# Input of the first expert tile summed in PSUM instead of gathered, and tile tables by matmuls, in a one-core attention and mixture-of-experts block

## The reference

```
h = x + concat([conv, attn]) @ W_o            # gated short convolution, latent attention
n = RMSNorm(h)
top 4 of 32 experts by n @ w_router + b_router; gates = softmax of the four
y[token] = sum over its experts: gate * expert(n[token])
expert(r) = act(r @ w_gate_up + b) @ w_down + b_down ;  out = h + y
```

## Time and profile before

| what | value |
|---|---|
| three runs | 2205.37, 2206.23, 2207.76 us (median 2206.23) |
| profiled execution | 2206.78 us; its span 2205.0 us |
| PE busy | 2078.0 us, 94% of the span |
| granted PE clock, mean | 0.976 of full speed |

### The profile page before, as it was taken

One profiled execution on the slowest core, in us unless ns is written; L12 is line 12 of the kernel. 1 busy time (PEld: TensorE's weight loads), 2 busy tenths in 40 slices (PEclk: granted clock), 3 DMA queues, 4 the chain that ended last, 5 costly groups with the idle time before them and its releaser, 6 DMA issues.

```text
span 2205.0 us, 41908 instructions
## 1 busy us (share of the span) xinstructions
PE 2078.0 (94%) x15574; PEld 1883.0 (85%) x15575; DVE 738.2 (33%) x1949; ACT 443.7 (20%) x1078; POOL 563.1 (26%) x645
## 2 busy tenths in 40 slices
PE   7999999999968899999999999999999999999991
PEld 6777777745538899999999999999999999999991
DVE  1322333233443334234333333333233332343331
ACT  1333323232311111111111111111111111111110
POOL 2211111100233223322222322323223233232321
PEclk9999999999978999999999999999999999999996
DMA  7100000242517889999899999999999999999987
GB/s 251 40 10 11 10 11 1 80 131 47 145 39 228 268 281 310 313 297 304 270 305 277 310 289 298 310 284 289 301 312 318 308 272 283 321 315 319 306 284 88
DMA packets 305892, 486.97 MB, mean 221 GB/s; under 512 B 105920, under 2 KB 127200, under 8 KB 305792
## 3 DMA queue, kind: packets, MB, share of 16 engines
q1 hardware_dynamic: 247184, 437.28, 60.6%
q0 software_dynamic: 33376, 45.11, 9.9%
q10 hardware_dynamic: 25280, 3.85, 1.1%
HBM read 454.83 MB, written 35.84 MB: 223 GB/s over the span
## 4 chain that ended last, share of the span: by engine, by line
PE 91%; issue 2%; DVE 2%; ACT 1%; DMA 1%; POOL 1%; ACTq 0%; DVEq 0%; SPq 0%; POOLq 0%
PE psum L1003 43%; PE psum L1019 22%; PE psum L803 8%; PE psum L952 5%; PE psum L842 3%; PE psum L911 2%; PE psum L820 2%; PE psum L910 1%; PE psum L884 1%; PE psum L932 1%; PE psum L895 1%; DMA area<-in_w_in 1%; PE psum L982 1%; DVE area L1302 0%; DVE area L1297 0%
## 5 line engine op out<-in xcount | busy, mean ns | idle before, releaser
L1003 PE MATMUL psum<-area 128*128 128x128 f32 (+3 forms) x8192 | 980.2, 282 | 37.0 <-issue 18.9
L1003 PEld LDWEIGHTS psum<-area 128*128 128x128 f32 x8192 | 971.6, 192 | 42.4 <-issue 42.4
L1019 PE MATMUL psum<-area 128*128 128x128 f32 (+3 forms) x4096 | 496.4, 282 | 0.9
L1019 PEld LDWEIGHTS psum<-area 128*128 128x128 f32 x4096 | 484.5, 191 | 10.0 <-DVE area L1302 8.7
L1283 DVE TENSOR_SCALAR area<-psum,area 128x160 f32<-128x160 f32 x256 | 86.4, 380 | 615.6 <-PE psum L1003 615.6
L600 POOL DMA_INDIRECT sum_rows<-area x165 | 264.0, 1600 | 67.4 <-issue 40.2
L762 ACT ACTIVATE area<-area 128x320 f32<-128x320 f32 x128 | 60.4, 472 | 735.8 <-DVE area L1283 735.6
L803 PE MATMUL psum<-area 128*128 128x128 f32 x1536 | 176.8, 276 | 10.5 <-ACT area L681 4.0
L803 PEld LDWEIGHTS psum<-area 128*128 128x128 f32 x1536 | 173.3, 192 | 15.3 <-ACT area L677 5.8
L590 POOL DMA_INDIRECT area<-normed_rows,area x165 | 161.3, 977 | 61.5 <-issue 61.5
L585 POOL TENSOR_TENSOR area<-area 128x5 uint32<-128x5 uint32 x33 | 6.3, 190 | 617.4 <-DVE area L1268 590.4
(11 more groups left out here) (184 smaller groups left out, 1250.6 us busy)
## 6 DMA issues: line engine op xcount, KB each, us to landing
area<-in_w_gate_up SPq DMA_DIRECT2D x256, 1024.0 KB, 6.4
area<-in_w_down SPq DMA_DIRECT2D x128, 1024.0 KB
area<-in_w_in SPq DMA_DIRECT2D x3, 2048.0 KB, 21.5
area<-in_x SPq DMA_DIRECT2D x9, 512.0 KB, 4.0
area<-in_w_o SPq DMA_DIRECT2D x1, 4096.0 KB, 13.0
sum_rows<-area SPq DMA_DIRECT2D x32, 128.0 KB
normed_rows<-area SPq DMA_DIRECT2D x8, 512.0 KB, 3.1
out<-sum_rows SPq DMA_DIRECT2D x4, 1024.0 KB, 14.0
```

Of the source, the lines that this page charges most:

```text
L1003: ins = mm(dst, w_gu[piece][:, k, c * P:(c + 1) * P], xT[:, PART * s + k, 0:width], start=(s == 0 and k == 0 and c % 2 == 0), stop=(s == 1 ...
L1019: ins = mm(bank[4 + d // 3][:, (d % 3) * SLOTS:(d % 3) * SLOTS + width], w_dn[q][:, kk, d * P:(d + 1) * P], actT[:, 2 * q + kk, 0:width], ...
```

## The change

Tile 0 is now always expert 0's first tile (`levels` and `floor` see to that when it is empty), and its input is no longer gathered from DRAM after the tables. Three parts are summed in PSUM banks 4 to 6, already transposed: rows of blocks 0 to 5, read from DRAM early by two indirect gathers with list entries read while block 7 is in work, and multiplied by the identity (`GTa`, `GTb`); and rows of blocks 6 and 7, straight from SBUF, multiplied by a 0/1 matrix that says which token takes which slot (`XTa`, `XTb`, `XT`). ACT and DVE copy the sum into `xT`. The last block's rows get a buffer of their own, `hf_last`, made after the `HB` copy. The last block's `places`, and with it POOL's list writes, come after the tables. The number of tiles an expert needs comes from a comparison with a row of levels, and the sums over experts from one matmul with a triangular 0/1 table, `upto`. The semaphore `gathered` becomes one for each of the five gathers. SP's branch on the first expert goes, and the early weights signal PE's semaphores themselves.

```diff
-                    ("HA", e), ("HB", e), ("RT", e), ("RK", e)]
+                    ("HA", e), ("XTa", e - 1), ("HB", e), ("XTb", e - 1), ("RT", e), ("GTa", e), ("RK", e), ("GTb", e), ("XT", e)]
...
                 b = i % H_ROWS
+                if i == NT - 1:
+                    sp.wait_ge(listed, 16 * (NT - DIRECT) * TOPK)
+                    for c, (a, m) in enumerate(FIRST):
+                        sp.dma_start(early_list[0:m, c, :], lists[a:a + m, :]).then_inc(early_in, 16)
...
+            wait(pv_done, NT * HEADS)
+            for c, (a, m) in enumerate(FIRST):
+                g.memset(early_rows[c][0:m, :], 0.0).then_inc(early_picked, 1)
             for n in range(NT):
+                if n == NT - DIRECT:
+                    wait(early_in, 16 * 2)
+                    for c, (a, m) in enumerate(FIRST):
+                        g.tensor_scalar(early_pick[0:m, c:c + 1], early_list[0:m, c, 0:1], 1.0 / Q, None, ALU.mult).then_inc(early_picked, 1)
+                    wait(early_picked, 2 + len(FIRST))
+                    wait(hf_out, 16 * (NT - DIRECT))
+                    for c, (a, m) in enumerate(FIRST):
+                        g.indirect_dma_start(early_rows[c][0:m, :], None, hf_dram[0:(NT - DIRECT) * P, :], bass.IndirectOffsetOnAxis(
+                            ap=early_pick[0:m, c:c + 1], axis=0), bounds_check=(NT - DIRECT) * P - 1, oob_is_err=False).then_inc(early_gathered, 16)
                 wait(place_ready, n + 1)
                 for k in range(TOPK):
                     g.indirect_dma_start(lists, bass.IndirectOffsetOnAxis(ap=put4[:, n, k:k + 1], axis=0),
...
-            gather(0)
+            take_rows(0)
...
+            act.wait_ge(first_done, 2)
+            for b in range(2):
+                A(xT[:, 3 * b:3 * b + 3, :], bank[4 + b][:, 0:3 * SLOTS].rearrange("p (k n) -> p k n", k=3), ACT.Copy).then_inc(first_copied, 1)
...
+                if kind in ("XTa", "XTb", "XT"):
+                    pe.wait_ge(placed, n - (NT - DIRECT) + 1)
+                    if n == NT - 1:
+                        pe.wait_ge(hf_ready, NT)
+                    rows_of = hf if n < NT - 1 else hf_last
+                    for d in {"XTa": range(KD // 2), "XTb": range(KD // 2, KD), "XT": range(KD)}[kind]:
+                        ins = mm(bank[4 + d // 3][:, (d % 3) * SLOTS:(d % 3 + 1) * SLOTS], rows_of.rearrange("t (p k) -> t k p", k=KD)[:, d, :],
+                                 is_place[:, n - (NT - DIRECT), :], start=(kind != "XT" and d % 3 == 0), stop=(kind == "XT"),
+                                 skip_group_check=True)
+                    if kind != "XTa":
+                        ins.then_inc(first_done, 1)
+                if kind in ("GTa", "GTb"):
+                    pe.wait_ge(early_gathered, 16 * 2)
+                    c = 0 if kind == "GTa" else 1
+                    a, m = FIRST[c]
+                    for d in range(KD):
+                        mm(bank[4 + d // 3][:, (d % 3) * SLOTS + a:(d % 3) * SLOTS + a + m], early_rows[c][0:m, :].rearrange("t (p k) -> t k p", k=KD)[:, d, :],
+                           ident[0:m, 0:m], start=False, stop=False, skip_group_check=True)
+                if kind == "RK" and n == NT - 1:
+                    pe.wait_ge(mask_ready, NT)
+                    mm(bank[3][0:E, 0:1], cums[:, NT, :], ones[:, 0:1], start=True, stop=True).then_inc(count_mm, 1)
                 if kind == "RK":
-                    rank_of(n, bank[4 + n - (NT - 2)][:, 0:E]).then_inc(rank_mm, 1)
-
-            mm(bank[6][:, 0:E], ones, cums[:, NT, :], start=True, stop=True).then_inc(rank_mm, 1)
+                    rank_of(n, bank[4 if n < NT - 1 else 1][:, 0:E]).then_inc(rank_mm, 1)
+                if kind == "GTb":
+                    mm(bank[0][:, 2 * E:3 * E], ones, cums[:, NT, :], start=True, stop=True)
+                    pe.wait_ge(used_ready, 1)
+                    mm(bank[0][:, 0:2 * E], used_b[0:E, :], K["upto"][0:E, :], start=True, stop=True).then_inc(total_mm, 1)
+
...
+            pe.wait_ge(first_copied, 2)
...
+                    if n == NT - 1:
+                        V.scalar_tensor_tensor(hf_last, h_sb[n % H_ROWS], rs_h[:, n:n + 1], gf_row,
+                                               ALU.mult, ALU.mult).then_inc(hf_ready, 1)
...
                 if kind == "RK":
-                    dve.wait_ge(rank_mm, n - (NT - 2) + 1)
-                    ch.link(V.tensor_tensor(rank_at, bank[4 + n - (NT - 2)][:, 0:E], K["room"], ALU.add))
+                    j = n - (NT - DIRECT)
+                    if j == 0:
+                        dve.wait_ge(lanes_in, 16)
+                    ch.link(V.tensor_scalar(off_list[:, j:j + 1], mask[:, n, 0:1], -OUTSIDE, OUTSIDE, ALU.mult, ALU.add))
+                if kind == "RK" and n == NT - 1:
+                    dve.wait_ge(count_mm, 1)
+                    ch.link(V.tensor_copy(count_c[0:E, :], bank[3][0:E, 0:1]))
+                    ch.link(V.tensor_scalar(over[0:E, :], K["levels"][0:E, :], count_c[0:E, 0:1], None, ALU.is_lt))
+                    ch.link(V.tensor_reduce(used_c[0:E, :], over[0:E, :], AX_X, ALU.add))
+                    V.tensor_copy(used_b[0:E, :], used_c[0:E, 0:1].to_broadcast([E, P])).then_inc(used_ready, 1)
+                if kind == "RK":
+                    dve.wait_ge(rank_mm, j + 1)
+                    ch.link(V.tensor_tensor(rank_at, bank[4 if n < NT - 1 else 1][:, 0:E], K["room"], ALU.add))
+                    V.tensor_scalar(is_place[:, j, :], lane_at, rank_at[:, 0:1], off_list[:, j:j + 1],
+                                    ALU.subtract, ALU.is_equal).then_inc(placed, 1)
+                if kind == "RK" and n < NT - 1:
                     places(n)
 
 
-            dve.wait_ge(rank_mm, 3)
-            dve.wait_ge(hf_out, 16 * NT)
-            dve.wait_ge(h_out, 16 * Q * NT)
-            ch.link(V.tensor_copy(count, bank[6][:, 0:E]))
-            ch.link(V.tensor_scalar(used, count, 0.0, None, ALU.is_gt))
-            for j in range(1, LEVELS):
-                ch.link(V.scalar_tensor_tensor(used, count, float(j * SLOTS), used, ALU.is_gt, ALU.add))
-            ch.link(V.tensor_copy(cum[:, 0, :], used))
-            src, s = 0, 1
-            while s < E:
-                V.tensor_copy(cum[:, 1 - src, 0:s], cum[:, src, 0:s])
-                ch.link(V.tensor_tensor(cum[:, 1 - src, s:], cum[:, src, s:], cum[:, src, 0:E - s], ALU.add))
-                src, s = 1 - src, 2 * s
-            total = cum[:, src, :]
-
-
-            tile_no = K["tokp"]
-            ch.link(V.tensor_tensor(first_t, total, used, ALU.subtract))
+            dve.wait_ge(total_mm, 1)
+            tile_no, total = K["tokp"], bank[0][:, 0:E]
+            V.tensor_copy(n_i, total[:, E - 1:E])
             V.tensor_scalar(past_e, total, tile_no, None, ALU.is_le)
-            ch.link(V.tensor_scalar(at_e, first_t, tile_no, None, ALU.is_le))
+            ch.link(V.tensor_scalar(at_e, bank[0][:, E:2 * E], tile_no, None, ALU.is_le))
             V.tensor_reduce(tab[:, 0:1], past_e, AX_X, ALU.add)
-            V.tensor_tensor(prod[:, 0, :], past_e, used, ALU.mult)
             ch.link(V.tensor_tensor(at_e, at_e, past_e, ALU.subtract))
-            V.tensor_reduce(tab[:, 1:2], prod[:, 0, :], AX_X, ALU.add)
-            ch.link(V.tensor_tensor(prod[:, 1, :], at_e, count, ALU.mult))
-            ch.link(V.tensor_reduce(tab[:, 2:3], prod[:, 1, :], AX_X, ALU.add))
+            ch.link(V.tensor_tensor(prod, mid(at_e, 2), bank[0][:, E:3 * E].rearrange("p (c e) -> p c e", c=2), ALU.mult))
             V.tensor_scalar(tab[:, 0:1], tab[:, 0:1], float(E - 1), None, ALU.min)
+            ch.link(V.tensor_reduce(tab[:, 1:3], prod, AX_X, ALU.add))
...
+            dve.wait_ge(first_done, 2)
+            V.tensor_copy(xT[:, 6:8, :], bank[6][:, 0:2 * SLOTS].rearrange("p (k n) -> p k n", k=2)).then_inc(xT_ready, 1)
+            places(NT - 1)
...
-            xT_out(0)
```

More of the change, by code:

```diff
@@ L64 @@
 ROOM = LEVELS * SLOTS
+OUTSIDE = 4096.0
+DIRECT = 2
 LISTED = E * ROOM
@@ L89, in constants @@
     }
+    e = np.arange(E, dtype=np.float32)
+    parts["levels"] = np.tile(np.arange(LEVELS, dtype=np.float32) * SLOTS, (P, 1))
+    parts["levels"][0, 0] = -1.0
+    parts["floor"] = np.where(p == 0, 1.0, -1.0e6)
+    parts["upto"] = np.concatenate([p <= e[None, :], p < e[None, :]], 1).astype(np.float32)
     at, where = 0, {}
@@ L101, in empty_lists, with lane_places @@
     return entry
+def lane_places():
+    return np.tile(np.arange(SLOTS, dtype=np.float32), (P, 1))
 def schedule():
@@ L310, in build @@
         put4 = take(NT, TOPK).bitcast(U32)
+        count_c, over, used_c, used_b = take(1), take(LEVELS), take(1), take(P)
         idx8 = idx8.bitcast(U32)
@@ L388, in build @@
         w_exp_in = [sem(f"w_exp_in{s}") for s in range(PIECES)]
-        early_in = sem("early_in")
-        gathered = sem("gathered")
+        gathered = [sem(f"gathered{k}") for k in range(G)]
         xT_ready = sem("xT_ready")
@@ L479, in _ @@
```

(2 more changed lines are left out.)

58 lines of the change are left out of this document (32 added, 26 removed).

## The result

The changed kernel took 2213.99 us (median of 8 runs, 2212.02 to 2218.34), the kernel before 2207.64 us (8 runs, 2205.37 to 2211.20): a ratio of 1.0029 [1.0019, 1.0039], so slower by 6.4 us. Forecast was 2195.2, in a range of 2187 to 2202. The profiled execution took 2212.02 us, with a span of 2210.2 us against 2205.0.

What follows compares the result with a forecast made beforehand. PE's 17.80 us idle stretch between router and first expert tile was taken as the bound. Gains of 3.4 us up to the tables and 9.6 us after, less 2.0 given back, made 11.0: 2195.2 us, range 2187 to 2202.

Steps and rivals of the forecast that it cites:

- T: End of the cast that publishes the tables: 654.44 before, forecast 651.0, with 648.6 and 653.5 as ends.
- What bounds the kernel now: PE holds 91% of the chain of waits; its longest idle stretch, 17.80 us before the first expert tile, is attacked.
- Before T: Last router block: router done 1.7 us earlier, at 640.0, despite eight 160-wide placing matmuls at 0.28 us; last mask at 642.4.
- rival (c): New matmuls on PE are slow because they read rows with a step of eight numbers: gain 5, 2201 us; chance 0.10.
- From the mask to T: Count, rank and table steps plus queued placing matmuls, 10.3 us before; T at 651.0, a gain of 3.4 us.
- From T to the down projection: Chain of list writes, list read, clearing and sigmoids takes 25.0 us, first down projection at 676.0; 9.6 us gained here.
- Given back: Slow PE clock after idling 5 to 8 us ahead of tile 0's down projection: 2.0 us lost (ends 0 and 3).
- Rival (a): The start chain to the sigmoids doesn't bind and tile 0 runs through: gain 18.4, 2188 us; chance 0.14.
- Rival (b): Code fetching moves: one PE stall of 5 us more or less at tile starts, 2190.5 or 2200.5; chance 0.12.
- Rival (d): Early gather lands late and holds PE's queue ahead of the count; slower than before once later than 652; chance 0.04.

Runs made afterwards that it cites:

- e8: Changed kernel with last block's places before the tables, copied operands in straight order, 30 tiny matmuls shifting loop code, last block's gates behind the count: 2191.18 us against 2208.13.
- e2: Changed kernel with placing and early-row matmuls reading plain slices of 128 neighbouring numbers, permuting tile 0's inputs: 2209.11 us against 2207.47 for the kernel before.
- e1: Changed kernel with the last block's places, and so POOL's list writes, put back ahead of the tables: 2204.50 us against 2207.47 for the kernel before.
- e4: Kernel before with 35 tiny matmuls (140 PE instructions) ahead of the tile loop: 2216.07 us against 2208.59 for the kernel before.
- e9: Changed kernel with 30 tiny matmuls (120 PE instructions) ahead of the tile loop: 2208.54 us against 2208.59 for the kernel before.
- e3: Changed kernel with both the last block's places ahead of the tables and plain-slice operands: 2197.87 us against 2207.47 for the kernel before.
- e7: Changed kernel with last block's places ahead of the tables and operands read from copies ACT and DVE put in straight order: 2200.20 us against 2208.59 for kernel before.

## Why the prediction was wrong

I forecast a gain of 11.0 us, and 6.4 were lost. By the spans the miss is 16.2 us (2210.2 instead of 2194.0), and the places named in the traces account for it: T 7.0, T to the down projection 2.7, the slow down projection 0.5, longer stalls and passes at tiles 1 and 2 about 0.7, the stall at 1009 with its slow passes 6.0, together 16.9, less 0.6 for a shorter tail behind the last down projection.

**What bounds the kernel now: right.** The wait that the change attacks was on the path: with the three losses of the changed kernel taken away (slow placing, late places, third stall), e8 is 16 us faster than before.

**Before T: the step that failed.** "A 160-wide matmul costs 0.28 us" was read from expert tiles, whose operands lie in order. The row was right and was not a row for this operation: PE took 0.525 us at full clock, and the ones over early rows doubled as well. That is rival (c), to which I gave 0.10. Its size came out right (T forecast at 657 under it, 658.0 measured), partly by luck, for I had placed the cost wrongly: it is worst where plain slices run at full clock (XTa, XTb, GTa, GTb) and small at the low clock (4.66 against 4.06 for the last placing), where I had put it. With plain slices T is 652.0, so the rest of the sum for T holds to 1 us as a whole. One term in it was misread: I priced the router's 16 passes at 1.0 us at full clock, but the row of 1.85 us at the low level is 8 passes, and all 16 took 1.87 us at full clock.

**From the mask to T: the same step again.** I had checked that PE would be through with GTa before the count needs it, at 0.22 us a matmul. At 0.52 GTa held the count for 1.5 us, and GTb, at 4.01 us, held the totals. With plain slices both waits go: in e2 PE is idle for 0.67 us until the mask releases the count.

**From T to the down projection: right in kind, one term short.** The idle stretch, its releaser, the table load behind the clearing and the start of tile 0 all came as forecast. The list read was taken as 4.35 us from a quiet stretch, and 7.3 us was measured. The refills that ran beside it are a consequence of tile 0 starting early: PE freed its buffers sooner. e1 has the read ahead of the refills and measures 3.65 us where the changed kernel, counted alike, has 6.6, and all thirteen traces split by this order. That the refills are what lengthens it is how they are best read together; no run varied them alone.

**Given back: 2.0 forecast, 2.5 measured** (9.94 for 7.41). e1 removed it by removing the wait.

**Rival (a)** did not hold in the changed kernel, and e1 made it true by one line of order.

**Rival (b): right in kind, too low a chance on its bad side.** I gave it 0.12, half to each side. It cost 6.1 us, because the stall brings slow passes with it (15.90 for 14.55), which I had not priced. e4 shows it in the kernel before and e9 removes it from the changed one. (b) and (c) both coming true was a case I did not price at all; by the traces they cost 6.1 and 6.5 us, together more than the 11.0 that I expected to gain.

**Rival (d)** was wrong: PE didn't wait for the early gather, and ran from the router into GTa without a wait (642.02).

**What stays open.** Why the third stall depends on the loop's place: shifts of 0, 8 and 258 instructions don't have it, 138 and 140 do. These few points bound no rule. e8, with another 258-odd, agrees with e9 but changes much else. Nor is it known what lengthens the stall before tile 1 to 7.9 us in e2 and 7.7 in e3, what lets tile 0 run at full clock in e3 and e8 but not in e7, or what moves the output projection by up to 5 us from one trace to another.

## What to carry to other kernels

When work moves to another engine, price it from a row with the same layout of operands, not only the same shape; if there is none, take at least the worst factor that any engine shows for that layout as likely (DVE showed 1.5 here, PE paid 2.0). When a wait is removed, follow the chain of every other engine that must be done by the next meeting point, and put its slowest links (here four list writes and a list read) ahead of what they don't depend on. And a change in a long program moves code: compare the stalls released by "issue" at tile starts between both traces before judging the change itself, and pad to tell them apart.

## What the runs showed of the hardware

- Eight float32 matmuls whose stationary operand is 128 numbers read with a step of 32 bytes took twice as long at full clock (4.05 us in e9 against 2.03 in e2), while a step of 8 bytes cost 6% (2.16). Four that are 160 wide took 2.05 us with a step of 16 bytes and 2.10 with one of 32, against 1.25.
- The strided ones took as long at a granted clock of 0.50 as at 1.00 (3.94 and 4.01 us against 4.01 and 4.05). Where the clock was mostly 0.50 the step cost only 15% (4.66 against 4.06 us for sixteen passes 160 wide).
- A stall of some 5 us at a tile's start came with 138 or 140 PE instructions more ahead of the loop and went with 258. In each such stall one 16 KB block of code was fetched. The two earlier ones, before tiles 1 and 2, came in every kernel (4.8 to 7.9 us).
- The last transfer of a list read (four DMAs) took 1.74 us in the kernel before and 5.00 us in the changed one, where four 1 MB weight loads ran beside it.
- Putting rows of 1024 float32 numbers in another order took ACT 2.0 us a copy (4.02 for the two of e7).
